# Layer 1 projections of a hybrid decoder step: keys and values alternate by pieces of 256 columns

## What is computed

```
proj = _rmsnorm(x, norm_g) @ w_in            # 1024 -> 4*1024 + 16
q, k, v, g, f = split(proj)
q = _rmsnorm(q per head, q_g); k = _rmsnorm(k per head, k_g)
logf = log_sigmoid(f + b_f)
sample groups: s = q . k_all  over 4096 past keys, fetched page by page (page_table)
```

## Time and profile before

| | |
|---|---|
| time, median of 3 runs | 3198.45 us (3194.75 to 3200.6) |
| profiled execution: its time / its span | 3206.94 us / 3205.4 us |
| PE, DVE, ACT, POOL busy over the span | 88%, 50%, 32%, 43% |
| first and last matmul of the 128 units | 1026.7 and 1896.5 us |
| mean granted TensorE clock | 0.950 |

### The profile page before, as it was taken

The page is one execution under the profiler, slowest core; times in us unless marked ns, Lnnn a source line. Parts: engine busy times, 40 slices in busy tenths (PEclk is TensorE's granted clock), DMA queues, the critical chain, the costliest instruction groups (busy, mean ns, idle before and its releaser), DMA issues. The chain is left out here.

```text
span 3205.4 us, 46935 instructions
## 1 busy us (share of the span) xinstructions
PE 2827.6 (88%) x17133; PEld 2246.4 (70%) x17133; DVE 1608.6 (50%) x2154; ACT 1024.0 (32%) x1721; POOL 1381.3 (43%) x986
## 2 busy tenths in 40 slices
PE   3887979695998999889999965999999999999999
PEld 2887868683774998879899963555555555554787
DVE  4222223234365678888555536455555555553432
ACT  4323132322245222212112211444454544544100
POOL 0000000001000477667888853777777777777000
PEclk9998989897998999989999986999999999999899
DMA  4101010104563688879777756977878878874532
GB/s 122 35 21 40 20 40 20 40 13 147 175 184 117 195 263 280 257 256 292 256 255 238 255 172 145 251 206 224 240 218 224 238 209 235 227 217 131 179 118 74
DMA packets 327904, 547.51 MB, mean 171 GB/s; under 512 B 76093, under 2 KB 220129, under 8 KB 319212
## 3 DMA queue, kind: packets, MB, share of 16 engines
q1 hardware_dynamic: 263564, 471.12, 50.0%
q10 hardware_dynamic: 61120, 58.83, 5.3%
q0 software_dynamic: 3008, 14.81, 1.3%
HBM read 449.58 MB, written 95.12 MB: 170 GB/s over the span
## 5 line engine op out<-in xcount | busy, mean ns | idle before, releaser
L1151 POOL TENSOR_TENSOR p_kp<-p_kp,p_qb 128x1024 f32<-128x1024 f32 x256 | 628.6, 2483 | 391.6 <-DMA p_kp<-in_cache_k_dram 313.3
L1997 POOL TENSOR_TENSOR at_acc<-at_acc,at_w 128x512 f32<-128x512 f32 (+3 forms) x576 | 644.8, 1119 | 231.1 <-ACT at_w L2125 165.4
L112 PE MATMUL p_pb<-p_w,x_xh 128*128 128x256 f32 x2048 | 595.0, 291 | 14.3 <-DVE p_w L1465 14.3
L2160 DVE TENSOR_REDUCE at_mx<-at_mx 128x1 f32<-128x512 f32 (+3 forms) x640 | 382.5, 608 | 425.7 <-PE at_mx L2032 312.0
L113 PE MATMUL p_pb<-p_w,x_xh 128*128 128x256 f32 x2048 | 582.3, 284 | 0.0
L114 PE MATMUL p_pb<-p_w,x_xl 128*128 128x256 f32 x2048 | 581.6, 284 | 0.0
L2125 ACT ACTIVATE at_w<-at_st,c_nckt 128x512 f32<-128x512 f32 (+3 forms) x640 | 389.5, 622 | 365.8 <-PE at_st L2058 193.4
L1567 DVE TENSOR_REDUCE p_sc<-p_kp 128x16 f32<-128x1024 f32 x256 | 308.2, 1215 | 230.6 <-POOL p_kp L1151 230.5
L112 PEld LDWEIGHTS p_pb<-p_w,x_xh 128*128 128x128 f32 x2048 | 393.6, 192 | 26.7 <-DVE p_w L1465 15.4
L113 PEld LDWEIGHTS p_pb<-p_w,x_xh 128*128 128x128 f32 x2048 | 395.5, 193 | 0.0
L114 PEld LDWEIGHTS p_pb<-p_w,x_xl 128*128 128x128 f32 x2048 | 394.6, 193 | 0.0
(11 more groups left out here) (296 smaller groups left out, 3837.2 us busy)
## 6 DMA issues: line engine op xcount, KB each, us to landing
p_kp<-in_cache_k_dram SPq DMA_DIRECT2D x256, 512.0 KB, 4.9
at_vp<-in_cache_v_dram SPq DMA_DIRECT2D x256, 512.0 KB, 5.4
o_mt<-mixed SPq DMA_DIRECT2D x32, 512.0 KB, 4.9
p_raw<-in_w_in_dram SPq DMA_DIRECT2D x32, 512.0 KB, 7.3
at_q<-qh SPq DMA_DIRECT2D x32, 512.0 KB, 10.7
at_k<-kh SPq DMA_DIRECT2D x32, 512.0 KB, 8.3
l_raw<-in_w_in_dram SPq DMA_DIRECT2D x20, 512.0 KB
mixed<-l_w POOLq DMA_DIRECT2D x8, 1028.0 KB, 4.2
```

Source lines behind the costliest of these rows:

```text
L112: nc.tensor.matmul(out, lhs[0], rhs[0], start=(k == 0), stop=False)
L1151: nc.gpsimd.tensor_tensor(kp[:, g % 4], kp[:, g % 4], qb[:], ALU.mult).then_inc(kmul, 1)
L1997: nc.gpsimd.tensor_tensor(t[:, 512 - wd:512], t[:, 512 - wd:512], W[n % RW][:, 0:wd], ALU.add).then_inc(accd, 1)
L2160: nc.vector.reduce_max(mx[:, u % 2, j, seg:seg + 1], MX[r % 2][:, 0:wd], AX.X).then_inc(mread, 1)
```

## The change

One line becomes two: the list of chunks is written as `ORDER`. Queries come first as before and g last; the eight chunks between them are k0 v0 k1 v1 k2 v2 k3 v3 in place of k0 k1 k2 k3 v0 v1 v2 v3. So chunks 4, 6, 8, 10 are keys (units 32 to 39, 48 to 55, 64 to 71, 80 to 87), and 5, 7, 9, 11 values. No instruction is added or taken away.

```diff
     KINDS = "qkvg"
-    CHUNKS = [(kind, i, KINDS.index(kind) * z.D + CWD * i) for kind in KINDS for i in range(NI)]
+    ORDER = [("q", i) for i in range(NI)] + [(kind, i) for i in range(NI) for kind in "kv"] + [("g", i) for i in range(NI)]
+    CHUNKS = [(kind, i, KINDS.index(kind) * z.D + CWD * i) for kind, i in ORDER]
     NCK = len(CHUNKS)
```

## The result

The changed kernel takes 3211.73 us (median of 6, 3208.3 to 3214.68); the ratio to the kernel before is 1.0033 (95% interval 1.002 to 1.0046). A second series of ten gave 3208.76 us and 1.0037 (1.0022 to 1.0051). So the change costs 0.2 to 0.5% by the two intervals, 6 to 16 us. The forecast of 3195.4 us was wrong, in size and in direction, and the measured time lies above its range. The kernel before had medians of 3196.8 to 3201.6 us in the series that follow; each ratio is against the executions of before on the same chip. One execution of a later experiment (both edits, new order) took 4117.48 us at a granted clock of 0.649 in place of about 0.94, and is left out of its series.

What follows compares the result with a forecast made beforehand. The prediction took DVE to bound keys and POOL values, not TensorE. Its terms, 0 - 2.6 + 0 - 0.4 = -3.0 us, took the median of 3198.45 to 3195.4 us, range 3179 to 3206.

Steps and rivals of the forecast that it cites:

- What bounds the kernel: Keys go at DVE's pace, values at POOL's; the stage's end moves as much as DVE's progress around unit 97.
- Step 1: Units 31 to 95, chunk lengths summed in the new order: 454.3 us against 454.3 before, so 0.
- Step 2: Value chunks of 18 pages: whether late pages recur is unknown; bounds 0 to -5.2 us, taken as -2.6.
- Steps 3 and 4: Three more edges from keys to values, taken as 0 us, and three more from values to keys, -0.4 us.
- step 4: Edges from values to keys: first two key units lack `lo`, mostly no saving; bounds -4.1 to 0, taken as -0.4 us.
- The rule weighed: A DVE instruction with two SBUF inputs waits out a running GpSimd instruction; for L1552 a few us at most.
- rival (b): Slower: at key-to-value edges DVE's wait for `hi` and two `lo` aren't hidden; +8.2 us in all, 3206.7 us; chance 0.12.
- Rival (a): POOL's four buffers full after keys, value chunks at its bare pace; 20.8 us less, 3177.7 us; chance 0.18.

Runs made afterwards that it cites:

- both edits, new order: Changed kernel with the keys' gain multiplied first on the PSUM buffer and the four small sample-key products replaced by reductions: 3178.50 us, ratio 0.9945 to before.

## Why the forecast was wrong

- **What bounds the kernel: right.** DVE and POOL set the stretch, and TensorE still stopped for `raw` at unit 101. That the end moves by as much as DVE's progress around unit 97 holds only in part: 5.6 us there were 3.6 at the last matmul. The pair without changes of sample shows the limit: when DVE is close behind, TensorE sets the end.
- **Step 1, the sum over chunks: this is the step that failed.** It took a key chunk's length as a property of the chunk (57.8 us) and a change of sample as a fixed wait to be added (9.1). The term for the three key chunks, 3 x (57.8 + 9.1) = 200.7 us, measured 209.1 and 207.6 in the two traces. The chunk's length contains the time for which DVE's instructions with two inputs in SBUF stand behind a running POOL, and that depends on what comes before them. In a key chunk behind values the first small product was long each time (3 of 3 in the trace of the change), behind keys in one or two of three in the traces of before. (That it was long because POOL was running is shown by the count above. Why POOL is running just then is argued, not shown: behind values it has no finished pages in hand and works whenever a page lands. Without changes of sample the square was long in all four chunks of the old order too.) With a change of sample at u = 2 POOL runs five pages at once exactly beside the next two small products. The fixed 9.1 was wrong for the change of sample behind unit 66: it cost DVE 12.38 and 11.86 us as it had cost 11.50 in the value chunk of before, so 2.1 to 2.6 of the 6.9 to 8.4 us come from there. The experiments bear out the collisions as a whole and not their split. The distance between the medians of the new and the old order, with a 95% interval from drawing the executions again:

| what is taken away | distance, us |
|---|---|
| nothing | 11.9 (8.2 to 14.7) |
| small products | 9.5 (3.8 to 13.8) |
| gain's second SBUF input | 8.5 (3.8 to 11.4) |
| the same, and the square | 4.7 (1.7 to 7.2) |
| gain's second SBUF input and all small products | 2.1 (-8.9 to 5.6) |

Neither edit alone levels the orders; both together do, as far as the width of the last interval lets one say.

- **Step 2, late pages: not wrong in sign, too hopeful.** Value chunks with 18 pages took 48.1 and 49.4 us, near the 49.0 of before; the -2.6 didn't come. In the second trace they took 47.6 each, so about that much came there.
- **Steps 3 and 4, edges: small, as taken.** DVE waited 0.7 us for ScalarE's `hi` over the whole stretch, less than the 2.8 of before. Two key units at each edge waited up to 0.37 us for ScalarE's root, 2.2 us in all, so about half of the 4.1 us of `lo` was lost again. That `lo` lies in steady keys where DVE waits for this root anyway, as step 4 has it, no row showed: DVE had no such wait in the keys of before.
- **The rule weighed and rival (b).** The row named the mechanism, and I priced it at "a few us at most" for L1552 alone. I had looked at the maximum of the largest instruction and not at the small products, whose time grows sixfold. In sum L1552 hardly changed between the orders (41.1 to 40.5 us, and 44.2 to 45.5). The rival had the right side and 0.12, but as to its mechanism that was luck: DVE stood 0.7 us for `hi`, where its price of 11.2 us came from that wait.
- **Rival (a), smoothing,** didn't come: the value chunks took 45 to 49 us, and not the 40.1 to 42.5 that it needs. Without changes of sample the new order was 8 us quicker, but its value chunks were as long.

Not settled: how the loss splits over the instructions. The pair with only the small products replaced was 9.5 us apart by its medians, while DVE's stretches in its traces are 1.6 us apart. It may be that the gains fall out worse in the new order in most executions, but no trace here shows that. Why the order with values first loses 8 us by its medians though its trace has the shorter stretch is open too. So is why POOL's gap for the query was 13.3 and 14.9 us in key chunks 8 and 10 and about 10 in value chunks.

## What to carry to other kernels

When work is only reordered, don't carry over a chunk's measured length: split it into the instructions' bare durations and what drew them out, and ask what each drawn-out part will stand beside in the new order. Look at the spread (min, median, max) of small instructions too, as a 0.4 us product can cost 2.6. Spreading one engine's load gained nothing here, as the chain that sets the end got longer by it; and taking one SBUF operand away from an instruction that stands beside GpSimd was worth more here (0.5%) than the order of the chunks. When single executions spread by 10 us, a difference of 10 us needs a series of each kernel, and the trace of a long execution needn't be that of a typical one.

## What the runs showed of the hardware

A product of 8 partitions by 256 took 0.41 us on DVE with GpSimd idle (43 of 43 in the four traces of before and of the change) and 2.4 to 2.6 us when it began beside GpSimd's product of 128 by 1024 (21 of 21); a reduction of the same size took 0.40 to 0.41 us each of 32 times, in the same places. The same gain of 128 by 512 took 0.69 to 2.9 us with both inputs in SBUF and 0.677 to 0.691 us with one of them in PSUM. Which of the small products is long is nearly the same in the two traces of the change (six of the eight long ones of the first, and no others, in the second), but not in those of before: three were long in one, four in the other, and only one in both. So the order fixes it in part, and chance has a part.
